# Spreading a row of token factors over the partitions: two small transfers through memory instead of a diagonal and matmuls with ones

## The chip, the cores and the metric

The kernel runs on one core of a Trainium2 chip. Its time is the device time of one launch in microseconds (us). The core has five engines with instruction streams of their own: TensorE (PE in the rows; PEld is its weight load), VectorE (DVE), ScalarE (ACT), GpSimd (POOL) and SyncE (SP), which here only issues transfers. They wait for one another by semaphores. Transfers between HBM and on-chip memory run on 16 DMA engines that all queues share; SP's transfers go out on one queue (q1) and those that GpSimd issues on another (q0).

## The reference, cut to what matters

Twelve sublayers follow one another on a stream `x` of 256 tokens by 1024 features, all in fp32. Each normalizes `x` by its root mean square, multiplies by matrices, normalizes the result and adds it to `x`:

```python
def rms_norm(x, g):
    y = x * rsqrt(mean(x * x, axis=-1, keepdims=True) + 1e-6)
    return y * g

# an FFN sublayer (8 of the 12); the others are one retention, one latent
# attention ("mla") and two mixers with stick-breaking attention ("stick")
h = rms_norm(x, g0)
f = (silu(h @ w_gate) * (h @ w_up)) @ w_down          # 1024 -> 2816 -> 1024
x = x + 0.5 * rms_norm(f, g1)
```

The factor `rsqrt(mean(x*x) + eps)` is one number for each token. It need not be applied to `h`: it may be applied after the first matrix product, since that product is linear in each token's row.

## The kernel before

**Layout.** The 256 tokens are two tiles (`T = 2`) of 128. Weights arrive in slots of 1 MB: `raw` holds three of them (`RING = 3`). For each slot ScalarE rounds it into `w_hi` (`high`, L929), VectorE takes the rest `raw - w_hi` into `w_lo` (`low`, L1317), and TensorE multiplies both parts, so that products of a two-part weight and a two-part activation (`h_hi`, `h_lo`) come near fp32. SP loads slot n + 3 once `low` of slot n is done. Every engine's stream is written out by hand in the order in which it runs; there is no planner.

**The token factor.** `h_hi` and `h_lo` hold `x` times the gain, without the token factor. ScalarE sums the squares of token tile t (`pre_sum`), GpSimd raises the mean to the power -0.5 (`pre_root`, L1825) into `stat[:, 4 + t]`, one number for each partition, tokens on partitions. Where a product has tokens on partitions, an engine applies the factor as a scalar of its instruction. Where a product has tokens along the row (`cols_of`, `gemm_pair`), the factor is needed as a row that is the same on all 128 partitions: `row_scale`, 128 x 256.

**How the row is made.** For the 11 sublayers that use it (all but the latent attention):
- VectorE, in `diag` (L1348): two 128 x 128 diagonals `row_diag` = identity times the factor, in the buffer `upd`. It is the last thing in `between`, the stretch between two sublayers; for sublayer 0 it stands before `low(6)`.
- TensorE, in `spread_scale` (L499): two fp32 matmuls of a matrix of ones with the diagonals, into `row_bank`, after the sublayer's first two slots (`first_slots`). They wait for `diag_ready`.
- ScalarE, in `row_copy` (L955): a copy of the bank to `row_scale`, after its `high(b + 3)` in an FFN sublayer, after the output of the second slot in the others.
- VectorE waits for `row_ready` before its first use: in an FFN sublayer the multiplication at L1502 in `gate(1)`, in the retention the scaling of the cosine table at L1631, in a stick sublayer the output of the third slot at L1731.

**An FFN sublayer on TensorE.** The first slots b and b + 1 (gate and up columns of chunk 0) come with tokens on partitions. Then `gemm_pair` on slot b + 2 (gate columns of chunk 1), four transposes at L680, `gemm_pair` on b + 3, `gemm_down` on b + 4, and a loop of chunks, each a gate pair, a down product and an up pair. The gate pair of chunk i + 1 waits for `gate_out` of chunk i, which VectorE gives at L1502.

**GpSimd's queue.** After the roots of sublayer 0 it computes the exponents of the retention's decay matrices, six times L1859, L1860 and L1861 on 128 x 512 elements, though they are not used before the retention. Then it loads gains. Between sublayers its order is: two roots of the update's norm (`post_root`), the load of the next `post_gain`, two roots of the next norm (`pre_root`), the load of `pre_gain` (L1832) for the sublayer after the next. In sublayer 0 VectorE computes the angles of the position tables (`angles`, L1446) between the first and the second chunk: 13 instructions, each waiting for the one before.

Of the kernel before, what the change touches and what calls it, by code (L numbers as in the profile page):

```python
# [17 lines left out]
P = 128  # L18
S = 256
T = S // P  # L20
# [77 lines left out]
def build(nc, ins, out):  # L98
# [3 lines left out]
    with ctx:  # L102
# [20 lines left out]
        row_scale = sb("row_scale", [P, S])  # L123
        row_diag = upd[:, 0:S].rearrange("p (a b) -> p a b", a=T)
        const = sb("const", [P, KEPT])
# [85 lines left out]
        up_parts = up_banks[:, :].rearrange("p (a b c) -> p a b c", a=2, b=2)  # L211
        row_bank, turn_bank = down[0][:, 0:S], down[1][:, 0:512]
        gemm_bank = [bank0, bank1]
# [16 lines left out]
        post_sq = sem("post_sq")  # L230
        diag_ready, row_mm, row_ready = sem("diag_ready"), sem("row_mm"), sem("row_ready")
        gate_side_out, gate_summed, up_side_out, up_out = (sem(n) for n in ("gate_side_out", "gate_summed", "up_side_out", "up_out"))
# [24 lines left out]
        pool_d, pool_mm, pool_hi, pool_lo = sem("pool_d"), sem("pool_mm"), sem("pool_hi"), sem("pool_lo")  # L257
        pool_w_zero = sem("pool_w_zero")

        block = ctx.enter_context(nc.Block())  # L260
# [143 lines left out]
        def _(pe):  # L404
# [93 lines left out]

            def spread_scale(u):  # L499

                pe.wait_ge(diag_ready, ROWS_BEFORE[u] + 1)
                for t in range(T):
                    last = mm(row_bank[:, t * P:(t + 1) * P], cst("ones"), row_diag[:, t, :], start=True, stop=True)
                last.then_inc(row_mm, 1)

            def down_of(n, k0, t, hi, lo, first, end, halves=range(2)):
# [152 lines left out]
            for u, kind in enumerate(SUBLAYERS):  # L659
                b = first_slot[u]  # L660
                if kind == "ffn":
                    e, g0, g1 = CHUNKS * ffns, (CHUNKS - 1) * ffns, (CHUNKS - 2) * ffns
                    first_slots(u + 1, [(b, bank0), (b + 1, bank1)], second=lambda: pe.wait_ge(evac, evacs[0]))
                    spread_scale(u)

# [31 lines left out]
                if kind == "ret":  # L697
                    mem = list(mem_heads(0, 0))
                    first_slots(u + 1, [(b + j, next_bank()) for j in range(2)])
                    spread_scale(u)  # L700
                    for j in range(2, N_RET):
# [86 lines left out]
                else:  # L788
# [35 lines left out]
                    first_slots(u + 1, [(b + j, next_bank()) for j in range(2)])  # L824
                    spread_scale(u)
                    for j in (2, 3):
# [80 lines left out]
        def _(sc):  # L907
# [43 lines left out]
            def scale_of(t):  # L951

                return stat[:, 4 + t:5 + t]

            def row_copy():  # L955

                rows[0] += 1
                sc.wait_ge(row_mm, rows[0])
                act_fn(row_scale[:, :], row_bank, ACT.Copy).then_inc(row_ready, 1)

            rows = [0]

# [123 lines left out]
            for u, kind in enumerate(SUBLAYERS):  # L1086
                b = first_slot[u]
                if kind == "ffn":
# [21 lines left out]
                    high(b + 3)  # L1110
                    row_copy()
                    high(b + 4)
# [30 lines left out]
                else:  # L1143
                    if kind == "ret":
# [19 lines left out]
                        for j in range(N_RET):  # L1164
                            steps((j, 0))
                            if 4 <= j < 10:

                                sc.wait_ge(slot_done, b + j + 1)
                                wait(sc, roped, j - 4)
                                bank = gemm_bank[evacs[0] % 2]  # L1170
                                act_fn(rope_sw[0:64, :], bank[64:P, :], ACT.Copy).then_inc(rope_swapped, 1)
                                act_fn(rope_sw[64:P, :], bank[0:64, :], ACT.Copy).then_inc(evac, 1)
                                evacs[0] += 1
                            elif j < 3:
                                rows_out(b + j, u, [(r_v[:, :, j * SC:(j + 1) * SC], 0, SC)])
                                if j == 1:
                                    row_copy()
# [68 lines left out]
                    else:  # L1246
                        c0 = 4 * sticks
                        for j in range(2):
                            rows_out(b + j, u, [(s_v[:, :, j * SC:(j + 1) * SC], 0, SC)])
                            if j == 1:  # L1250
                                row_copy()
                            high(b + j + 3)
# [60 lines left out]
        def _(ve):  # L1313
# [33 lines left out]

            def diag(u):  # L1348

                ve.wait_ge(pre_rs, 2 * (u + 1) + 2)  # L1350
                for t in range(T):
                    last = v.tensor_scalar(row_diag[:, t, :], ident, stat[:, 4 + t:5 + t], None, ALU.mult)
                last.then_inc(diag_ready, 1)

            def pre_low(p, t):
# [24 lines left out]
            def between(u):  # L1380
# [20 lines left out]
                low(b + 2)  # L1401
                if SUBLAYERS[u + 1] != "mla":
                    diag(u + 1)

# [78 lines left out]
            for t in range(T):  # L1483
                pre_low(1, t)
            diag(0)
            low(6)

            ffns, sticks = 0, 0
            for u, kind in enumerate(SUBLAYERS):
                b = first_slot[u]  # L1490
                if kind == "ffn":
                    e, g0, g1 = CHUNKS * ffns, (CHUNKS - 1) * ffns, (CHUNKS - 2) * ffns

                    def gate(i):
# [5 lines left out]
                        ve.wait_ge(gate_summed, g0 + i)  # L1500
                        ve.wait_ge(row_ready, ROWS_BEFORE[u] + 1)
                        v.tensor_tensor(sums, sums, row_scale[:, :].unsqueeze(1).broadcast_to([P, 2, S]), ALU.mult).then_inc(gate_out, 1)  # L1502
# [69 lines left out]
                else:  # L1572
                    if kind == "ret":
# [51 lines left out]
                        for j in range(N_RET):  # L1625
                            if j < 3:
                                low(b + j + 3)
                            if j == 1:
                                ve.wait_ge(table_ready, 1)
                                ve.wait_ge(row_ready, ROWS_BEFORE[u] + 1)  # L1630
                                v.tensor_tensor(trig[:, :, 0:S], trig[:, :, 0:S], row_scale[:, :].unsqueeze(1).broadcast_to([P, 2, S]),  # L1631
                                                ALU.mult).then_inc(trig_scaled, 1)
# [85 lines left out]
                    else:  # L1718
# [5 lines left out]
                        def slot_out(j):  # L1724
# [3 lines left out]
                            if j == 2:  # L1728
                                ve.wait_ge(row_ready, ROWS_BEFORE[u] + 1)
                            src = gemm_bank[(outs + j) % 2][:, :].rearrange("p (a b) -> p a b", a=2)  # L1730
# [87 lines left out]
        def _(gp):  # L1818
# [24 lines left out]
            def load_post_gain(u):  # L1843
                wait(gp, x_new, 4 * u)
                load_gain(post_gain, post_in, gain_row(u, 1))

            load_gain(post_gain, pre_in, ins["mem_norm"])
            gp.wait_ge(const_in, 16)
# [4 lines left out]
            for t in range(T):  # L1853
                pre_root(1, t)

            gp.wait_ge(small_in, SMALL_FIRST)
# [14 lines left out]
            for u, kind in enumerate(SUBLAYERS):  # L1871
# [65 lines left out]
```

## Time and profile before

| What | us |
|---|---|
| median of 3 runs (lowest and highest) | 1949.82 (1949.72 to 1950.51) |
| the profiled execution: its own time | 1949.68 |
| the profiled execution: span from first to last instruction | 1947.9 |
| TensorE busy (share of the span) | 1916.2 (98%) |
| VectorE busy | 1295.8 (67%) |
| ScalarE busy | 1032.6 (53%) |
| GpSimd busy | 158.4 (8%) |
| mean busy share of the DMA engines in the 40 slices of the span | 0.2 to 0.8, mostly 0.5 |

The granted clock of TensorE is at full speed in all 40 slices. Matmuls are pipelined and the profile models their ends, so the distance between starts tells more of their cost than the duration of one. "Idle" in the rows is time in which an engine stood still before an instruction, followed by what released it. In groups that name a line, a helper's line stands for all its callers.

### The profile page before, as it was taken

The numbers are of one execution on the slowest core, as the hardware profiler recorded it, in microseconds if no ns is written. First come the engines' busy times: TensorE is split into PE (matmuls) and PEld (weight loads), VectorE is DVE, ScalarE is ACT, GpSimd is POOL, SyncE is SP. The second block draws the span as 40 slices with busy tenths as digits, with TensorE's granted clock in tenths as the row PEclk, the third lists the DMA queues.
The fourth block names the chain that finished last, engine by engine and source line by source line (L and its number), as shares of the span: only waits on it lengthen the run. The fifth ranks groups of instructions, "written<-read, shape, count | busy, mean of one in ns | idle before, by whom it ended". The sixth has DMA issues, their size and how long they took to land.

```text
span 1947.9 us, 29001 instructions
## 1 busy us (share of the span) xinstructions
PE 1916.2 (98%) x11272; PEld 1685.9 (87%) x11272; DVE 1295.8 (67%) x1346; ACT 1032.6 (53%) x1190; POOL 158.4 (8%) x149
## 2 busy tenths in 40 slices
PE   6999999999999999999999999999999999999998
PEld 6888889888888887888888889888888888988887
DVE  4766756766676667666676666776667666667665
ACT  5544564544554457644464446654455445665443
POOL 2600113100000001100010001210001000300000
PEclk9999999999999999999999999999999999999999
DMA  8555553555555554455555556355555555535552
GB/s 303 195 194 194 179 164 134 195 194 193 175 201 186 190 167 139 145 203 194 188 180 196 190 187 205 112 192 197 191 194 195 173 193 196 195 130 182 184 187 104
DMA packets 262263, 356.25 MB, mean 183 GB/s; under 512 B 9008, under 2 KB 230576, under 8 KB 262192
## 3 DMA queue, kind: packets, MB, share of 16 engines
q1 hardware_dynamic: 258592, 342.15, 52.7%
q0 software_dynamic: 3600, 13.11, 1.8%
q8 instruction: 50, 0.82, 0.2%
q14 instruction: 21, 0.17, 0.0%
HBM read 354.19 MB, written 1.05 MB: 182 GB/s over the span
## 4 chain that ended last, share of the span: by engine, by line
PE 89%; DVE 4%; ACT 4%; issue 2%; DMA 1%; SPq 0%; POOL 0%; DVEq 0%; POOLq 0%; ACTq 0%
PE down L512 27%; PE gate_banks L435 15%; PE up_banks L435 14%; PE gate_banks L439 8%; PE up_banks L439 7%; PE up_banks L418 3%; PE up_banks L420 3%; PE up_banks L419 3%; PE up_banks L480 2%; ACT w_hi L940 1%; DVE w_lo L1327 1%; PE up_banks L471 1%; PE up_banks L472 1%; DVE xn L1345 1%; DMA raw<-in_ffn_w_gu 1%
## 5 line engine op out<-in xcount | busy, mean ns | idle before, releaser
L1321 DVE TENSOR_TENSOR w_lo<-raw,w_hi 128x2048 fp32r<-128x2048 f32 (+1 forms) x311 | 710.5, 2287 | 278.8 <-ACT w_hi L940 278.8
L940 ACT ACTIVATE w_hi<-raw 128x2048 fp32r<-128x2048 f32 x322 | 613.6, 1906 | 205.1 <-PE down L512 178.6
L435 PE MATMUL gate_banks<-h_both,w_hi 128*128 128x512 f32 x1280 | 321.0, 393 | 0.0
L435 PE MATMUL up_banks<-h_both,w_hi 128*128 128x512 f32 x1152 | 287.4, 391 | 0.0
L512 PE MATMUL down<-w_hi,m_hi 128*128 128x512 f32 x832 | 267.9, 394 | 0.0
L435 PEld LDWEIGHTS gate_banks<-h_both,w_hi 128*128 128x128 f32 x1280 | 230.6, 189 | 41.6
L512 PE MATMUL down<-w_lo,m_hi 128*128 128x512 f32 x832 | 264.8, 390 | 0.0
L512 PE MATMUL down<-w_hi,m_lo 128*128 128x512 f32 x832 | 264.4, 390 | 0.0
L435 PEld LDWEIGHTS up_banks<-h_both,w_hi 128*128 128x128 f32 x1152 | 211.1, 188 | 40.5
L439 PEld LDWEIGHTS gate_banks<-h_both,w_lo 128*128 128x128 f32 x1280 | 174.6, 190 | 12.5
L512 PEld LDWEIGHTS down<-w_hi,m_lo 128*128 128x128 f32 x832 | 156.2, 188 | 33.3
L512 PEld LDWEIGHTS down<-w_lo,m_hi 128*128 128x128 f32 x832 | 156.2, 188 | 33.1
L439 PE MATMUL gate_banks<-h_both,w_lo 128*128 128x256 f32 x1280 | 178.5, 282 | 0.0
L512 PEld LDWEIGHTS down<-w_hi,m_hi 128*128 128x128 f32 x832 | 150.8, 189 | 26.0 <-issue 0.3
L1093 ACT ACTIVATE big<-up_banks 128x512 f32<-128x512 f32 x72 | 43.3, 601 | 234.5 <-PE up_banks L439 234.5
L439 PEld LDWEIGHTS up_banks<-h_both,w_lo 128*128 128x128 f32 x1152 | 157.2, 190 | 11.2
L439 PE MATMUL up_banks<-h_both,w_lo 128*128 128x256 f32 x1152 | 160.6, 282 | 0.0
L418 PE MATMUL up_banks<-h_both,w_hi 128*128 128x256 f32 x512 | 147.2, 288 | 0.0
L419 PE MATMUL up_banks<-h_both,w_hi 128*128 128x256 f32 x512 | 144.8, 283 | 0.0
L420 PE MATMUL up_banks<-h_both,w_lo 128*128 128x256 f32 x512 | 144.8, 283 | 0.0
L1515 DVE TENSOR_TENSOR big<-up_banks,big 128x512 f32<-128x512 f32 x72 | 49.8, 691 | 123.0 <-ACT big L1093 123.0
L1829 POOL TENSOR_TENSOR stat<-stat,const 128x1 f32<-128x1 f32 x24 | 13.2, 552 | 1437.4 <-ACT stat L922 1437.4
(230 smaller groups left out, 2315.3 us busy)
## 6 DMA issues: line engine op xcount, KB each, us to landing
raw<-in_ffn_w_gu SPq DMA_DIRECT2D x88, 1024.0 KB, 5.0
raw<-in_ffn_w_down SPq DMA_DIRECT2D x88, 1024.0 KB, 4.9
raw<-in_ffn_w_gate SPq DMA_DIRECT2D x44, 1024.0 KB, 5.2
raw<-in_ffn_w_up SPq DMA_DIRECT2D x44, 1024.0 KB, 5.2
raw<-in_w_in SPq DMA_DIRECT2D x20, 1024.0 KB, 5.6
raw<-in_ret_w_in SPq DMA_DIRECT2D x13, 1024.0 KB, 5.2
raw<-in_w_o SPq DMA_DIRECT2D x8, 1024.0 KB, 4.9
raw<-in_w_out SPq DMA_DIRECT2D x8, 1024.0 KB, 4.7
```

The lines of the kernel that those rows point to most:

```text
L418: mm(o, w_hi[:, r, c:c + P], hi[:, k, :], start=(k == 0), stop=False)
L419: mm(o, w_hi[:, r, c:c + P], lo[:, k, :], start=False, stop=False)
L420: last = mm(o, w_lo[:, r, c:c + P], hi[:, k, :], start=False, stop=(k == KD - 1))
L435: mm(both, w_hi[:, r, c:c + P], h_both[:, k, :, :].rearrange("p a b -> p (a b)"), start=(k == 0), stop=(k == KD - 1), skip_group_check=True)
L439: last = mm(one, w_lo[:, r, c:c + P], h_hi[:, k, :], start=False, stop=(k == KD - 1), skip_group_check=True)
L471: mm(o, hi[:, k, ts], w_hi[:, n % RING, c:c + SC], start=(k == 0), stop=False)
L480: last = mm(o, hi[:, k, ts], w_lo[:, n % RING, c:c + SC], start=False, stop=(k == KD - 1))
L512: last = mm(down[t][:, c * 512:(c + 1) * 512], a[:, k0 + j, ts], w[:, r, j * D + c * 512:j * D + (c + 1) * 512], start=(first and j == 0 a ...
L940: act_fn(w_hi[:, r, 0:width], raw[:, r, 0:width], ACT.Copy).then_inc(hi_ready, 1)
L1093: act_fn(dst, parts[:, :, 1, :], ACT.Copy).then_inc(s, 1)
L1321: v.tensor_tensor(w_lo[:, r, 0:width], raw[:, r, 0:width], w_hi[:, r, 0:width].bitcast(f32), ALU.subtract).then_inc(lo_ready, 1)
L1515: v.tensor_tensor(sums, up_parts[:, :, 0, :], up_side, ALU.add).then_inc(up_out, 1)
```

## The change

The diagonals, the matmuls with ones and ScalarE's copy are gone, with their semaphores. In their place GpSimd issues two transfers, in `spread_rows`. The first writes the two columns of `stat`, 256 numbers on 128 partitions, to a row of 256 numbers in memory (HBM), 4 bytes at a time. GpSimd then waits for it to land (`row_put`) and issues the second, which reads that row of 1 KB onto each of the 128 partitions of `row_scale`. The consumers on VectorE stay where they were and wait for the second transfer.

```diff
-        row_diag = upd[:, 0:S].rearrange("p (a b) -> p a b", a=T)
...
+        row_store = nc.dram_tensor("row_store", (len(SUBLAYERS), S), f32, kind="Internal").ap()
...
-            def spread_scale(u):
-
-                pe.wait_ge(diag_ready, ROWS_BEFORE[u] + 1)
-                for t in range(T):
-                    last = mm(row_bank[:, t * P:(t + 1) * P], cst("ones"), row_diag[:, t, :], start=True, stop=True)
-                last.then_inc(row_mm, 1)
...
-            def row_copy():
-
-                rows[0] += 1
-                sc.wait_ge(row_mm, rows[0])
-                act_fn(row_scale[:, :], row_bank, ACT.Copy).then_inc(row_ready, 1)
...
-            def diag(u):
-
-                ve.wait_ge(pre_rs, 2 * (u + 1) + 2)
-                for t in range(T):
-                    last = v.tensor_scalar(row_diag[:, t, :], ident, stat[:, 4 + t:5 + t], None, ALU.mult)
-                last.then_inc(diag_ready, 1)
...
-                        ve.wait_ge(row_ready, ROWS_BEFORE[u] + 1)
+                        ve.wait_ge(row_ready, 16 * (ROWS_BEFORE[u] + 1))
...
+            def spread_rows(u):
+
+                gp.wait_ge(pre_rs, 2 * (u + 1) + 2)
+                gp.dma_start(row_store[u, :].rearrange("(t p) -> p t", p=P), stat[:, 4:4 + T], allow_slow_non_contiguous=True).then_inc(row_put, 16)
+                gp.wait_ge(row_put, 16 * (ROWS_BEFORE[u] + 1))
+                gp.dma_start(row_scale[:, :], row_store[u, :].partition_broadcast(P)).then_inc(row_ready, 16)
+
...
             for t in range(T):
                 pre_root(1, t)
+            spread_rows(0)
 
             gp.wait_ge(small_in, SMALL_FIRST)
             for h in range(HEADS_R):
...
                     pre_root(u + 2, 0)
                     pre_root(u + 2, 1)
+                if u + 1 < U and SUBLAYERS[u + 1] != "mla":
+                    spread_rows(u + 1)
                 if u + 2 < U:
                     load_pre_gain(u + 3)
```

The calls of `spread_scale`, `row_copy` and `diag` are removed at all their places. Two places in the instruction streams show what that does. On TensorE at the start of an FFN sublayer, before the change (L480 is the end of `first_slots`, L503 the matmuls with ones, L435 and L439 the first gate pair, L680 the transposes):

```order
L480 MATMUL up_banks<-w_lo,h_both 128x256 x8
L503 MATMUL down<-upd,const 128x128 x2
L435 MATMUL gate_banks<-h_both,w_hi 128x512 x8
L439 MATMUL gate_banks<-h_both,w_lo 128x256 x8
L435 MATMUL gate_banks<-h_both,w_hi 128x512 x8
L439 MATMUL gate_banks<-h_both,w_lo 128x256 x8
L680 MATMUL down<-const,big 128x128 x4
```

The same place after it:

```order
L481 MATMUL up_banks<-w_lo,h_both 128x256 x8
L436 MATMUL gate_banks<-h_both,w_hi 128x512 x8
L440 MATMUL gate_banks<-h_both,w_lo 128x256 x8
L436 MATMUL gate_banks<-h_both,w_hi 128x512 x8
L440 MATMUL gate_banks<-h_both,w_lo 128x256 x8
L673 MATMUL down<-const,big 128x128 x4
```

The two matmuls with ones are gone, and nothing else has moved. On GpSimd at the start of the program, between the roots of sublayer 0 and the decay exponents, before the change:

```order
L1832 DMA pre_gain<-in_norm_gains 128x1024 [waits pre_in]
L1825 TENSOR_TENSOR stat<-stat,const 128x1 [waits pre_ss] x2
L1859 TENSOR_SCALAR big<-big,lgd 128x512 [waits small_in]
L1860 TENSOR_SCALAR rope_t<-big,lgd 128x512
L1861 TENSOR_TENSOR big<-big,rope_t 128x512 [waits pool_link]
```

And after it:

```order
L1800 DMA pre_gain<-in_norm_gains 128x1024 [waits pre_in]
L1793 TENSOR_TENSOR stat<-stat,const 128x1 [waits pre_ss] x2
L1818 DMA row_store<-stat 128x2x1 [waits pre_rs]
L1820 DMA row_scale<-row_store 128x256 [waits row_put]
L1835 TENSOR_SCALAR big<-big,lgd 128x512 [waits small_in]
L1836 TENSOR_SCALAR rope_t<-big,lgd 128x512
L1837 TENSOR_TENSOR big<-big,rope_t 128x512 [waits pool_link]
```

The 18 instructions of the decay exponents now stand behind a wait for a transfer to land. At the other ten places the two transfers stand in the same way between the last root and the load of `pre_gain`.

## Rows read from the trace of the kernel before

**Rows 1.** Page, parts 1 and 4: busy time by engine; chain by engine.
```profile
PE 1916.2 (98%) x11272; PEld 1685.9 (87%) x11272; DVE 1295.8 (67%) x1346; ACT 1032.6 (53%) x1190; POOL 158.4 (8%) x149
...
PE 89%; DVE 4%; ACT 4%; issue 2%; DMA 1%; SPq 0%; POOL 0%; DVEq 0%; POOLq 0%; ACTq 0%
```
**Rows 2.** Waits of TensorE: line, releaser: us in total, times, longest.
```profile
PE up_banks L480 <- DVE w_lo L1327: 5.3, 11, 0.5
```
**Rows 3.** Chain that ended last, sublayer 3 (FFN): start us, us, what.
```profile
552.77 0.96 PE up_banks L480 x8
553.73 0.44 PE down L503 x4
554.18 1.85 PE gate_banks L435 x8
```
**Rows 4.** Timeline of GpSimd and VectorE, sublayer 3: start, us, engine, line, operation.
```profile
550.48 0.57 POOL L1832 DMA_DIRECT2D pre_gain<-in_norm_gains  x1
550.55 0.52 DVE L1352 TENSOR_SCALAR upd<-const,stat 128x128 f32<-128x128 f32 x2 [0.44 <-POOL stat L1825]
...
562.25 0.69 DVE L1502 TENSOR_TENSOR big<-big,row_scale 128x512 f32<-128x512 f32 x1
...
565.45 2.29 DVE L1321 TENSOR_TENSOR w_lo<-raw,w_hi 128x2048 fp32r<-128x2048 f32 x1 [2.50 <-ACT w_hi L940]
```
**Rows 5.** Timeline of TensorE, sublayer 3: start of the next chunk's gate pair.
```profile
571.11 1.98 PE L435 MATMUL gate_banks<-h_both,w_hi 128*128 128x512 f32 x8
```
**Rows 6.** Timeline, retention (first two) and first stick sublayer (last two).
```profile
240.06 0.57 POOL L1832 DMA_DIRECT2D pre_gain<-in_norm_gains  x1
...
250.97 0.68 DVE L1631 TENSOR_TENSOR trig<-trig,row_scale 128x512 f32<-128x512 f32 x1
...
1192.30 0.57 POOL L1832 DMA_DIRECT2D pre_gain<-in_norm_g  x1
...
1201.81 0.69 DVE L1731 SCALAR_TENSOR_TENSOR big<-up_banks,row_scale 128x512 f32<-128x512 f32 x1 [0.96 <-PE up_banks L420]
```
**Rows 7.** Page and DMA view, issues: count, KB each, median us to landing.
```profile
post_gain<-in_norm_gains POOLq DMA_DIRECT2D x6, 512.0 KB, 3.8
out<-x SPq DMA_DIRECT2D x4, 256.0 KB, 2.0
pos_row<-in_positions SPq DMA_DIRECT2D x1, 128.0 KB, 7.8
small<-in_conv_w SPq DMA_DIRECT2D x6, 1.0 KB, 4.5
pos_col<-in_positions SPq DMA_DIRECT2D x1, 1.0 KB, 7.6
```
**Rows 8.** Timeline of GpSimd and VectorE, sublayer 0: decay exponents and angles.
```profile
38.47 2.16 POOL L1859 TENSOR_SCALAR big<-big,lgd 128x512 f32<-128x512 f32 x1
...
64.41 1.57 POOL L1859 TENSOR_SCALAR big<-big,lgd 128x512 f32<-128x512 f32 x1
64.71 0.93 DVE L1502 TENSOR_TENSOR big<-big,row_scale 128x512 f32<-128x512 f32 x1
...
77.24 2.33 POOL L1861 TENSOR_TENSOR big<-big,rope_t 128x512 f32<-128x512 f32 x1
78.34 1.38 DVE L1450 CAST big<-pos_row 128x256 f32<-128x256 int32 x1
...
85.90 2.29 DVE L1321 TENSOR_TENSOR w_lo<-raw,w_hi 128x2048 fp32r<-128x2048 f32 x1
```
**Rows 9.** Timeline of TensorE, sublayer 0: the gate pair behind these angles.
```profile
90.15 2.00 PE L435 MATMUL gate_banks<-h_both,w_hi 128*128 128x512 f32 x8
```
**Rows 10.** Timeline, retention: GpSimd beside VectorE's tensor_scalar, and one alone.
```profile
265.03 1.31 POOL L1881 TENSOR_TENSOR big<-rope_t,rope_sw 128x512 f32<-128x512 f32 x1
265.43 1.33 DVE L1431 TENSOR_SCALAR big<-big,sm 128x256 f32<-128x256 f32 x2
...
268.68 0.62 DVE L1431 TENSOR_SCALAR big<-big,sm 128x256 f32<-128x256 f32 x2
```

More of the change, by code:

```diff
@@ L211, in build @@
         up_parts = up_banks[:, :].rearrange("p (a b c) -> p a b c", a=2, b=2)
-        row_bank, turn_bank = down[0][:, 0:S], down[1][:, 0:512]
+        turn_bank = down[1][:, 0:512]
         gemm_bank = [bank0, bank1]
@@ L230, in build @@
         post_sq = sem("post_sq")
-        diag_ready, row_mm, row_ready = sem("diag_ready"), sem("row_mm"), sem("row_ready")
+        row_put, row_ready = sem("row_put"), sem("row_ready")
         gate_side_out, gate_summed, up_side_out, up_out = (sem(n) for n in ("gate_side_out", "gate_summed", "up_side_out", "up_out"))
@@ L663, in _ @@
                     first_slots(u + 1, [(b, bank0), (b + 1, bank1)], second=lambda: pe.wait_ge(evac, evacs[0]))
-                    spread_scale(u)
                     def chunk(n, i, at=None):
@@ L699, in _ @@
                     first_slots(u + 1, [(b + j, next_bank()) for j in range(2)])
-                    spread_scale(u)
                     for j in range(2, N_RET):
@@ L824, in _ @@
                     first_slots(u + 1, [(b + j, next_bank()) for j in range(2)])
-                    spread_scale(u)
                     for j in (2, 3):
@@ L953, in scale_of @@
                 return stat[:, 4 + t:5 + t]
-            def row_copy():
-                rows[0] += 1
-                sc.wait_ge(row_mm, rows[0])
-                act_fn(row_scale[:, :], row_bank, ACT.Copy).then_inc(row_ready, 1)
-            rows = [0]
             def pre_high(p, t):
@@ L1110, in _ @@
                     high(b + 3)
-                    row_copy()
                     high(b + 4)
@@ L1175, in _ @@
                                 rows_out(b + j, u, [(r_v[:, :, j * SC:(j + 1) * SC], 0, SC)])
-                                if j == 1:
-                                    row_copy()
                             elif j == 3:
@@ L1249, in _ @@
                             rows_out(b + j, u, [(s_v[:, :, j * SC:(j + 1) * SC], 0, SC)])
-                            if j == 1:
-                                row_copy()
                             high(b + j + 3)
@@ L1401, in between @@
                 low(b + 2)
-                if SUBLAYERS[u + 1] != "mla":
-                    diag(u + 1)
             def head_low(head, banks=early):
@@ L1484, in _ @@
                 pre_low(1, t)
-            diag(0)
             low(6)
@@ L1629, in _ @@
                                 ve.wait_ge(table_ready, 1)
-                                ve.wait_ge(row_ready, ROWS_BEFORE[u] + 1)
+                                ve.wait_ge(row_ready, 16 * (ROWS_BEFORE[u] + 1))
                                 v.tensor_tensor(trig[:, :, 0:S], trig[:, :, 0:S], row_scale[:, :].unsqueeze(1).broadcast_to([P, 2, S]),
@@ L1728, in slot_out @@
                             if j == 2:
-                                ve.wait_ge(row_ready, ROWS_BEFORE[u] + 1)
+                                ve.wait_ge(row_ready, 16 * (ROWS_BEFORE[u] + 1))
                             src = gemm_bank[(outs + j) % 2][:, :].rearrange("p (a b) -> p a b", a=2)
```

## The prediction

> **What bounds the kernel now.** I read the page first, for who is busy. TensorE is busy for 1916.2 of 1947.9 us, and the chain of work that ended last runs on it for 89% [rows 1]: a microsecond taken from TensorE's stream is a microsecond of the kernel, unless something else then arrives late. Then TensorE's waits, for how close the others are. At the eleven boundaries between sublayers it waits 5.3 us in all for VectorE's half slots, at most 0.5 us at one place [rows 2]. Inside the sublayers its starts follow one another without gaps. Then the chain at the place of the change: the matmuls with ones stand in it directly between the last product of `first_slots` and the first gate product [rows 3]. The timelines of VectorE and GpSimd give the time from the last root to the first reader of `row_scale` [rows 4, 6]. Sublayer 0 I read apart, since only there GpSimd has other work behind the inserted transfers [rows 8].
>
> **What TensorE gains.** The chain gives the pair of fp32 matmuls (four records) 0.44 us [rows 3]. Nothing takes their place: the gate pair behind them needs slot b + 2, whose low part VectorE had finished before it turned to the diagonals at 550.55, 3 us before TensorE comes to them [rows 3, 4]. There are 8 FFN, 1 retention and 2 stick sublayers, so 11 x 0.44 = 4.8 us. The first gate product after the switch back from fp32 also starts a hundredth slower (1.85 us there); I take 4.9 us. The bounds are 0, if each pair's time were lost again at the next boundary, and 6.6 us, if each were worth its whole modelled duration of some 0.6 us. The chain is a row at this very place, so I stay by it. The removed diagonals (0.52 us on VectorE) and the copy on ScalarE were beside TensorE's work, and VectorE stands still behind them until TensorE ends a slot: 0, in either direction.
>
> **What the two transfers need, and what they have.** No row shows a store of 4-byte pieces or a read behind it. Nearest for the first is the load of 1 KB in 4-byte pieces, 4.5 us; its bounds are the large store of `out`, 2.0, and the 4-byte load in the flood of the start, 7.6. For the second, GpSimd's broadcast of 512 KB takes 3.8, and `pos_row`, the same shape as here but in that flood, 7.8 [rows 7]. Between ends so far apart I take 4.5 + 3.8 = 8.3 us, because the flood is over by then; both ends, 2.0 + 3.8 = 5.8 and 7.6 + 7.8 = 15.4, are kept.
>
> They start where `pre_gain` is loaded now. In an FFN sublayer that is 550.48, and VectorE reads the row at 562.25: 11.8 us [rows 4]. If it comes later, L1502, the rounding of the next slot and VectorE's low part, which ends at 565.45 + 2.29 = 567.74, move with it. TensorE wants them at 571.11 [rows 4, 5], so 3.4 us more are to be had, 15.1 in all. In the retention the reader comes 10.9 us after the start, in the stick sublayer 9.5 us [rows 6]. Behind that stick reader TensorE has another slot to multiply into the other bank, 48 products of 0.12 us (8 in 0.96, rows 3), 5.8 us more. So 8.3 us are hidden at all eleven places, 15.4 us would cost some tenths at each, about 3 us in all. I take 0.
>
> What queues behind GpSimd's wait: between sublayers only the load of `pre_gain`, which is issued some 5 us later and is first read a whole sublayer later. It will then share the DMA engines with another weight slot than now. The slots have one sublayer's pace of slack and the load takes 3.8 us alone [rows 7], so nothing.
>
> **Sublayer 0.** Here the 18 instructions of the decay exponents wait for the first transfer. They began at 38.47 [rows 8]; now they begin some 4.5 us later (2.0 to 7.6). One group of three takes 1.57 for each of the two `tensor_scalar` [rows 8] and 1.31 for a `tensor_tensor` of this size [rows 10], 4.4 us. So GpSimd runs one group late, and its last group, which ended at 77.24 + 2.33 = 79.57, falls under `angles`, VectorE's 13 dependent instructions that begin at 78.34 and keep the next gate waiting. The rows show what that costs. The `CAST` at 78.34 took 1.38 us and ended just after GpSimd's instruction [rows 8]; two `tensor_scalar` beside a GpSimd instruction took 1.33 instead of 0.62, and again ended as it did [rows 10]. Only L1502 beside a GpSimd `tensor_scalar` got off with 0.93 instead of 0.69 [rows 8 and 4]. So VectorE loses between 0.2 us and the whole of each GpSimd instruction that gets in. All three: 4.4 us, less the 1.2 us that the `CAST` pays already, 3.2 us. The low part of the slot behind the angles ends at 85.90 + 2.29 = 88.19; TensorE wants it at 90.15 [rows 8, 9], 0.45 us earlier now. The margin is 1.5 us. TensorE stalls 3.2 - 1.5 = 1.7 us, once, and does not get it back, since it bounds all that follows. The bounds: 0 when only tenths are lost, and 4.4 + 3.1 - 1.2 - 1.5 = 4.8 us when the first transfer takes 7.6 and the whole delay of GpSimd falls on VectorE.
>
> The Trainium skill, SBUF — State Buffer, section Who interferes with whom, says that a VectorE instruction in a two-port mode and a GpSimd instruction exclude each other for the whole instruction, and that a VectorE instruction with two SBUF inputs is held by a GpSimd instruction that reads SBUF. By that rule all three instructions count in full, and the stall is 1.7 us or more. The `CAST` and the paired `tensor_scalar` agree with it, L1502 beside the `tensor_scalar`, held for 0.24 us only, does not.
>
> **The sum.** 1949.68 (the profiled execution, 1.8 above its span and 0.14 below the median of the runs) - 4.9 + 0 + 1.7 = 1946.5 us. Its own range, with the stall from 0.5 to 3.2, is 1945.2 to 1948.0.
>
> **The rivals.**
> - Clean saving. GpSimd's delay is absorbed before the angles, or its instructions get in between VectorE's without holding them beyond the margin of 1.5 us: 1949.7 - 4.9 = 1944.8. For it speaks L1502's small loss, and that GpSimd's instructions also stretch wherever VectorE keeps it out. Against it, that the last group ended only at 79.57 with no delay at all.
> - The saving does not arrive. TensorE comes 0.44 us earlier to each boundary and waits there for VectorE's half slot that much longer [rows 2]; with the stall of sublayer 0 the time is 1949.7 to 1951.4. Against it: those half slots follow from TensorE's own last products, so they move with it.
> - Slower, by one mechanism: the pair of transfers outlasts the slack and VectorE's wait at L1502 holds up the gate pair of the second chunk in each FFN sublayer. It decides from 15.1 us for the pair on; each microsecond above costs 11, since the other three places have about as much, and 15.6 us take back the whole gain. At 20 us, if each transfer waited out a weight slot in flight, the time is 1949.7 - 4.9 + 11 x 4.9 = 1999. For it speaks that both 1 KB loads of the start took 7.6 and 7.8 [rows 7]; against it, that in the flood they had several megabytes in front of them.
>
> **How the numbers follow.** My forecast has 0.57, the clean saving 0.27, the lost saving 0.08, the outlasted slack 0.08. A change under 0.2%, 3.9 us, can't be told from none here: the border is 1945.9. The forecast's range reaches across it, with about 0.13 of its chance; with the clean saving that makes faster 0.40. Within 0.2% are the rest of the forecast, 0.44, and 0.07 of the lost saving and 0.01 of a barely outlasted slack: 0.52. Slower has 0.08. The range: 1944.5 takes in the clean saving, and 1948.6 the forecast with the stall at 3.7 and a little over; above it stay the lost saving and the slower case with part of the bound of 4.8.
>
> **What would show it.** Right: four records fewer between `first_slots` and the gate pair at each of the eleven places, and the next product 0.44 us sooner; no idle time of VectorE before L1502's successor put down to a transfer; both transfers landed within 8 us or so; in sublayer 0 decay exponents that still run at 80 us, a span of the angles longer than now, and TensorE idle for 1 to 3 us before the gate pair near 90 us. Wrong: idle time before the first reader of `row_scale` released by a transfer, or a sublayer 0 that is shorter by 0.44 us like the others; then the stall was priced too high. If the boundaries grow, the saving was no saving.

## The result

| Kernel | us, median (lowest to highest) | span of the profiled execution | mean granted clock in it |
|---|---|---|---|
| before | 1949.94 (1949.61 to 1950.51, 6 runs) | 1947.9 | 1.000 |
| after | 2002.92 (1998.35 to 2004.02, 6 runs) | 2000.4 | 0.988 |

The change made the kernel slower: the ratio is 1.0269, 95% interval 1.0259 to 1.0279. The prediction of 1946.5 us was wrong, in sign and far outside its range. What happened is its last rival, to which it gave 0.08.

### The profile page after: what moved, and what is told of

It is laid out like the page before. It is cut to its first block, busy times and chain, and to the rows that moved or that the text cites. A ratio compares the mean times of both kernels' runs of the same rounds, so it can differ in the third digit from the quotient of the medians.

```text
span 2000.4 us, 28902 instructions
## 1 busy us (share of the span) xinstructions
PE 1932.7 (97%) x11228; PEld 1696.4 (85%) x11228; DVE 1292.6 (65%) x1324; ACT 1027.6 (51%) x1179; POOL 172.4 (9%) x171
## 4 chain that ended last, share of the span: by engine, by line
PE 80%; DMA 9%; DVE 4%; ACT 4%; issue 2%; POOL 1%; DVEq 0%; SPq 0%; POOLq 0%; ACTq 0%
PE down L506 25%; PE gate_banks L436 14%; PE up_banks L436 12%; PE gate_banks L440 7%; PE up_banks L440 6%; DMA row_store<-stat 5%; DMA row_scale<-row_store 3%; PE up_banks L419 3%; PE up_banks L420 2%; PE up_banks L421 2%; DVE w_lo L1299 1%; PE up_banks L472 1%; PE up_banks L473 1%; POOL stat L1793 1%; ACT w_hi L931 1%
## 5 line engine op out<-in xcount | busy, mean ns | idle before, releaser
L436 PE MATMUL gate_banks<-h_both,w_hi 128*128 128x512 f32 x1280 | 332.4, 403 | 25.5 <-DVE w_lo L1299 25.5
L436 PEld LDWEIGHTS gate_banks<-h_both,w_hi 128*128 128x128 f32 x1280 | 237.9, 195 | 72.3 <-DVE w_lo L1299 28.7
L419 PE MATMUL up_banks<-h_both,w_hi 128*128 128x256 f32 x512 | 149.8, 292 | 9.6 <-DVE big L1699 9.6
L420 PE MATMUL up_banks<-h_both,w_hi 128*128 128x256 f32 x512 | 147.1, 287 | 0.0
```

What stands on the lines that cost most here:

```text
L419: mm(o, w_hi[:, r, c:c + P], hi[:, k, :], start=(k == 0), stop=False)
L420: mm(o, w_hi[:, r, c:c + P], lo[:, k, :], start=False, stop=False)
L436: mm(both, w_hi[:, r, c:c + P], h_both[:, k, :, :].rearrange("p a b -> p (a b)"), start=(k == 0), stop=(k == KD - 1), skip_group_check=True)
```

## The profile after

The page, parts 1 and 4, against [rows 1]:

```profile
PE 1932.7 (97%) x11228; PEld 1696.4 (85%) x11228; DVE 1292.6 (65%) x1324; ACT 1027.6 (51%) x1179; POOL 172.4 (9%) x171
...
PE 80%; DMA 9%; DVE 4%; ACT 4%; issue 2%; POOL 1%; DVEq 0%; SPq 0%; POOLq 0%; ACTq 0%
```

TensorE has 44 records fewer and yet 16.5 us more of busy time, so some of its work ran slower. The chain has a new member, DMA with 9%, taken from PE. The DMA issues of the two transfers (count, KB each, median us to landing) stand against [rows 7]:

```profile
row_scale<-row_store POOLq DMA_DIRECT2D x11, 128.0 KB, 6.6
row_store<-stat POOLq DMA_DIRECT2D x11, 1.0 KB, 10.8
```

The store alone takes longer than the prediction gave the pair. From the issue of the store to the landing of the read it is 17.0 to 18.5 us at the eleven places. The waits (who for whom: us in total, times, longest) show where that ends, beside [rows 2]:

```profile
POOL row_scale L1820 <- DMA row_store<-stat: 114.7, 11, 11.2
DVE big L1470 <- DMA row_scale<-row_store: 48.4, 7, 7.4
PE gate_banks L436 <- DVE w_lo L1299: 25.5, 8, 3.9
DVE big L1699 <- DMA row_scale<-row_store: 21.1, 2, 10.7
...
PE up_banks L419 <- DVE big L1699: 9.6, 2, 4.9
...
PE up_banks L481 <- DVE w_lo L1305: 5.3, 11, 0.5
```

The last row is [rows 2] unchanged: the boundaries are what they were. The third one is new, and so is the one of L419, the same wait in the two stick sublayers. In the retention TensorE stands still for 1.30 us at a place where it did not before (L566). Sublayer 3 as a timeline, against [rows 4, 5]:

```profile
560.61 0.75 POOL L1818 DMA_DIRECT2D row_store<-stat  x1 [0.29 <-POOL stat L1793]
571.48 0.57 POOL L1820 DMA_DIRECT2D row_scale<-row_store  x1 [10.12 <-DMA row_store<-stat]
578.96 0.69 DVE L1470 TENSOR_TENSOR big<-big,row_scale 128x512 f32<-128x512 f32 x1 [7.39 <-DMA row_scale<-row_store]
582.15 2.29 DVE L1299 TENSOR_TENSOR w_lo<-raw,w_hi 128x2048 fp32r<-128x2048 f32 x1 [2.50 <-ACT w_hi L931]
584.50 3.65 PE L436 MATMUL gate_banks<-h_both,w_hi 128*128 128x512 f32 x8 [3.87 <-DVE w_lo L1299]
588.96 2.00 PE L436 MATMUL gate_banks<-h_both,w_hi 128*128 128x512 f32 x8
```

The chain is the one that the prediction drew: store, read, L1470 (L1502 before), the rounding, the low part, the gate pair. The row arrives 18.3 us after the store's issue, 3.2 more than the slack of 15.1. TensorE idles 3.87 us, and then its first eight products take 3.65 us instead of 2.00. The windows of the same place (PE, PEld, DVE, ACT, POOL busy; then granted clock, DMA share, GB/s) say why:

```profile
565.00:570.00 5.00, 5.00 (x33) 4.54 (x32) 3.93 (x2) 1.39 (x3) 0.00 (x0) 1.00 0.53 26
...
580.00:585.00 5.00, 1.13 (x5) 0.59 (x4) 2.85 (x3) 4.40 (x4) 0.00 (x0) 0.97 0.15 53
585.00:590.00 5.00, 5.00 (x21) 4.14 (x20) 4.96 (x6) 2.44 (x2) 0.00 (x0) 0.69 0.67 216
590.00:595.00 5.00, 5.00 (x28) 4.27 (x27) 3.37 (x4) 2.92 (x3) 0.00 (x0) 1.00 0.97 341
```
```profile
586.00:588.00 2.00, 2.00 (x7) 1.51 (x6) 2.00 (x2) 1.59 (x2) 0.00 (x0) 0.50 0.96 326
```

After the idle time the granted clock is at 0.50 (1.2 GHz), and then at full speed again. The first row holds the other surprise. While the store is under way, the DMA engines are busy for 0.53 of the time and move 26 GB/s. The weight slot issued in that time, and the one behind it, landed after 9.4 and 12.8 us instead of some 5.

The lengths of the sublayers (from one first `post_root` to the next, minus those of before, in us) show how even the loss is. I use them for the experiments too:

```
sublayer      0     1     2     3     4     5     6     7     8     9    10    11
kind        ffn   ret   ffn   ffn   mla   ffn   ffn stick   ffn   ffn stick   ffn
after      1.72  2.42  5.65  5.30  0.02  5.60  6.17  6.56  4.96  3.97  6.06  3.85
```

They sum to 52.3; the spans differ by 52.5. The latent attention, which uses no row, has not changed.

## The experiments

Runs of before beside the timed ones had medians of 1949.95 to 1950.10 us. "Theory A" is that the store is slow by itself, wherever it is issued, and that the wait for the row is the loss.

**The store from ScalarE's queue.** In `spread_rows` the store goes; ScalarE issues it at the end of `between`:

```diff
-                gp.dma_start(row_store[u, :].rearrange("(t p) -> p t", p=P), stat[:, 4:4 + T], ...).then_inc(row_put, 16)
+                sc.dma_start(row_store[u, :].rearrange("(t p) -> p t", p=P), stat[:, 4:4 + T], ...).then_inc(row_put, 16)
```

> The kernel after, but ScalarE's queue issues the store of 256 four-byte pieces, at the same point of time; the read stays with GpSimd. Theory A (the store itself is slow to land, whoever issues it): the store still lands 10 to 11 us after its issue, GpSimd waits about as long, time 1995 to 2005. Rival B (GpSimd's queue makes it slow): it lands in 4 to 5 us as the 4-byte loads of before did, the pair needs 11 to 12 us, less than the slack of 15.1, and the time is 1945 to 1950.

Measured: 1993.12 us, ratio 1.0223 (1.0206 to 1.0240). Its DMA issues:

```profile
row_scale<-row_store POOLq DMA_DIRECT2D x11, 128.0 KB, 6.8
row_store<-stat ACTq DMA_DIRECT2D x11, 1.0 KB, 10.4
```

The store lands as late, so the queue is not the cause. The 10 us gained are more than theory A allowed. The pairs take 17.5 us on average instead of 17.9, and ScalarE issues the store some 0.3 us earlier against TensorE's stream. In the seven FFN sublayers 2 to 11 the second gate pairs come 19.6 us later in sum where they came 25.0 us later in the kernel after, and the slow clock behind them costs 10.3 us instead of 13.5. That is 8.5 of the 10.8 us between the two spans.

**The store alone, and the pair, beside the old way.** The kernel before keeps its diagonals and matmuls; GpSimd issues the store as well, in the second kernel both transfers into a spare buffer:

```diff
+                gp.dma_start(row_store[u, :].rearrange("(t p) -> p t", p=P), stat[:, 4:4 + T], ...).then_inc(row_put, 16)
+                gp.wait_ge(row_put, 16 * (ROWS_BEFORE[u] + 1))                            # the second kernel only
+                gp.dma_start(spare, row_store[u, :].partition_broadcast(P)).then_inc(...)  # the second kernel only
```

> The kernel before, its diagonals, matmuls with ones and copy kept, and GpSimd issues the store as well, which nobody reads (it waits for it before the next post_root only). If the store holds up the weight transfers enough to matter by itself (theory A2), slots issued beside it land in 9 to 13 us, ScalarE waits for them, and the time is 1955 to 1975. If all the harm comes by the wait for the row (theory A1): 1949 to 1952, with late slots that nobody misses.

> The kernel before, its own way to the row kept, and both transfers issued by GpSimd as in the kernel after, with its wait between them; they fill a spare buffer that nobody reads. A1 (the wait for the row is all): 1950 to 1953, of which about 2 are sublayer 0, where GpSimd's decay exponents start 11 us later and meet the angles. A2 (interference with the weights, or the later load of pre_gain): 1960 or more.

Measured: 1950.88 us (ratio 1.0004, 0.9995 to 1.0014) and 1951.78 us (1.0009, 0.9999 to 1.0018). The store still lands after 10.9 and 10.6 us, and the DMA issue rows of the first kernel at sublayer 3 show weights and gain late beside it:

```profile
raw<-in_ffn_w_gu SPq DMA_DIRECT2D x2, 1024.0 KB, 9.1
raw<-in_ffn_w_down SPq DMA_DIRECT2D x1, 1024.0 KB, 9.4
pre_gain<-in_norm_gains POOLq DMA_DIRECT2D x1, 512.0 KB, 11.6
row_store<-stat POOLq DMA_DIRECT2D x1, 1.0 KB, 11.6
```

No sublayer grows by more than 0.13 us with the store and, beyond sublayer 0 (0.54), by 0.10 with the pair. So late weights by themselves cost next to nothing here: the loss is the wait for the row, with what follows from it.

**Pieces of 8 bytes.** The row is stored token-major, 128 pieces of 8 bytes; VectorE reads it with a stride, in two instructions for each one of the kernel after:

```diff
-                gp.dma_start(row_store[u, :].rearrange("(t p) -> p t", p=P), stat[:, 4:4 + T], ...)
+                gp.dma_start(row_store[u, :].rearrange("(p t) -> p t", t=T), stat[:, 4:4 + T])
```

> The kernel after, with the row stored token-major, as 128 pieces of 8 bytes in place of 256 of 4; VectorE reads row_scale with a stride of 8 bytes, in two instructions for each one of after. If the store's landing time goes by the piece (the pieces landing one after another, some 21 ns each), it falls from 10.8 to about 8 us, the pair to 15.5, at the slack of 15.1, and the time is 1946 to 1965. If it is a fixed time, 10.8 stays and the time is 1998 to 2008.

Measured: 1948.93 us, ratio 0.9993 (0.9983 to 1.0003), 54 us less than after. The store takes 6.0 to 7.1 us until the read is issued, the pair 11.3 to 14.5. The longest pair, at sublayer 3, tests the slack of 15.1 and outlasts it: VectorE waits 3.62 us, TensorE stands still for 0.18 before the gate pair, which starts 0.34 us later for it and takes 2.12 instead of 1.98. This sublayer is 0.04 us longer than before where most are 0.45 shorter.

```profile
558.30 0.54 POOL L1831 DMA_DIRECT2D row_scale<-row_store  x1 [6.55 <-DMA row_store<-stat]
565.74 0.76 DVE L1299 TENSOR_TENSOR big<-big,row_scale 128x256 f32<-128x256 f32 x2 [3.62 <-DMA row_scale<-row_store]
571.36 2.12 PE L436 MATMUL gate_banks<-h_both,w_hi 128*128 128x512 f32 x8 [0.18 <-DVE w_lo L1306]
```

**Forms of the store, and of the read.** Two kernels with the old way to the row and, at each boundary, one transfer that nobody needs. The edit is that of the first; the second reads the 256 positions, a row of 1 KB, onto 128 partitions, in turn from GpSimd's and ScalarE's queue:

```diff
-                gp.dma_start(row_store[u, :].rearrange("(t p) -> p t", p=P), stat[:, 4:4 + T], ...)
+                dst, src = stores[PLAN[u]]              # another form at each boundary
+                gp.dma_start(dst, src, ...)
```

> The kernel before, and at each of the twelve boundaries one unneeded store from GpSimd's queue at the place of after's, of another form: 256, 512 and 128 pieces of 4 bytes, 128 pieces of 8 bytes, 256 pieces of 4 bytes set 64 or 512 bytes apart, 128 pieces of 64 bytes, one piece of 1 KB, and 128 pieces of 8 bytes into on-chip memory. By the piece: 512 pieces land after 15 to 17 us, 256 after 10.8 however far apart, 128 after about 8, one piece after about 5. By the line of memory that neighbouring pieces share: those 512 bytes apart land as fast as one piece. Fixed: all land near 10.8. The time stays within 1949.5 to 1953.

> The kernel before, and at each boundary one unneeded read of a row of 1 KB onto 128 partitions, without a store ahead of it: in turn from GpSimd's queue and from ScalarE's. If the store makes the read behind it slow, GpSimd's read lands in 3.8 to 4.5 us here and not in 6.6. If the read is as slow by itself, beside a weight slot, 6 to 7 us. ScalarE's queue: 3 to 5 us if GpSimd's queue is what delays the first packet, as long as GpSimd's if it is the slot in flight. The time stays within 1949.5 to 1953.

Issues of the store kernel. The trace leaves digits out of names: `p256x`, `p512x` and `p128x` of 0.5 KB are pieces of 4 bytes, `p128x` of 1 KB pieces of 8 bytes, of 8 KB pieces of 64 bytes, `apart` pieces of 4 bytes 64 and 512 bytes apart, `pos_row` the on-chip target.

```profile
p256x<-const POOLq DMA_DIRECT2D x2, 1.0 KB, 9.8
p128x<-const POOLq DMA_DIRECT2D x2, 1.0 KB, 7.3
p512x<-const POOLq DMA_DIRECT2D x2, 2.0 KB, 11.1
apart<-const POOLq DMA_DIRECT2D x2, 1.0 KB, 5.2
p128x<-const POOLq DMA_DIRECT2D x1, 0.5 KB, 9.8
one1k<-const POOLq DMA_DIRECT2D x1, 1.0 KB, 6.0
p128x<-const POOLq DMA_DIRECT2D x1, 8.0 KB, 5.4
pos_row<-const POOLq DMA_DIRECT2D x1, 1.0 KB, 5.3
```

"By the piece" falls: 128 pieces of 4 bytes take as long as 256, and the same 256 pieces take half as long when they lie 64 bytes apart or more. "Fixed" falls too. What makes the store slow is that its 4-byte pieces lie close together in HBM. The trace's DMA packets narrow down where the time goes. In the kernel after, the 16 packets on record for a store take at most 0.03 us each and the last one begins 3.3 to 6.7 us after the issue; then 3.7 to 7.4 us pass until the landing is told. In the kernel of store forms it is 4.2 to 6.6 us for the touching 4-byte pieces, 0.7 and 3.0 for the pieces of 8 bytes and 0.4 to 0.8 for all other forms. So the extra time lies behind the last packet.

The read of 1 KB onto 128 partitions took a median of 5.8 us from GpSimd's queue and 5.5 from ScalarE's, without a store ahead of it; in the kernel after it took 6.6. So the read is slow by itself, mostly, and the queue hardly matters. Times: 1950.87 and 1951.03 us, one run each.

**How close is close.** The same kernel, with other gaps and widths, and a second time with repeats of the forms in between:

```diff
-        PLAN = [the forms above]
+        PLAN = ["touching", "gap_eight", "gap_sixteen", "gap_thirtytwo", "piece_sixteen", "gap_sixtyfour", ...]
```

> The kernel before with one unneeded store at each of the twelve boundaries, as in the earlier kernel of store forms: 256 pieces of 4 bytes that touch, or begin 8, 16, 32 or 64 bytes apart, and 128 pieces of 16 or 32 bytes that touch. Theory L (pieces that fall into the same 64 bytes of memory wait for one another, about 0.29 us each, while different 64 bytes go side by side): over the 5.2 us of pieces 64 bytes apart, 16 pieces in 64 bytes add 4.6 us (landing 9.8), 8 (gap of 8) 2.3 (7.5), 4 (gap of 16, pieces of 16) 1.2 (6.4), 2 (gap of 32, pieces of 32) 0.6 (5.8). Rival (any piece under 64 bytes is slow where it touches its neighbour, gaps of any width are free): touching 4-byte pieces 9.8, all gaps 5.2, pieces of 16 and 32 bytes 6 to 8.

> The kernel before with one unneeded store at each boundary, again, for repeats of the forms in between: 256 pieces of 4 bytes that touch (two places), 128 pieces of 8 bytes that touch (four), 256 pieces of 4 bytes that begin 8 bytes apart (three) and 16 bytes apart (three). If only the number of pieces in the same 64 bytes counts (16, 8, 8 and 4), pieces of 8 bytes and gaps of 8 land alike, about 6.8 us, and gaps of 16 in 5.5 to 6. If it counts that pieces touch, pieces of 8 bytes land in 6.7 to 8 and both gaps in 5 to 6.4. Touching 4-byte pieces: 9.3 to 10.3 in both.

Each landing of the three kernels, in us, by how many pieces fall into the same 64 bytes of HBM:

```
pieces in 64 bytes   form                              landings
16                   4 bytes, touching (128 to 256)    9.3 9.3 9.4 9.7 9.8 10.3 10.7
 8                   8 bytes, touching                 5.8 6.0 6.2 6.6 6.7 7.9
 8                   4 bytes, every 8                  5.8 5.8 6.3 6.4 7.1
 4                   4 bytes every 16; 16 bytes        4.9 5.2 5.3 5.8 6.9; 4.5 5.3
 1 or 2              4 bytes every 32, 64, 512;        4.9 5.5 4.6 4.8 5.9;
                     32 or 64 bytes                    6.0; 5.4
```

Pieces of 8 bytes and gaps of 8 are alike (medians 6.4 and 6.3), so it is not that pieces touch: the number that share a neighbourhood counts. Theory L as I had put it, 0.29 us for each piece, does not hold: over the median of 5.3 us of the last two groups, 16 pieces add 4.4, 8 add 1.0, and 4 nothing that stands out of the spread of 2.4 us. What is awaited behind the last packet these traces don't show, nor whether 64 bytes is the unit. Times: 1951.70 and 1950.68 us, one run each.

**Filling the idle time.** The kernel after, with products that nobody reads in the place of the idle time:

```diff
+                    if u:
+                        pe.wait_ge(gate_summed, g0 + 1)
+                        for k in range(16):
+                            mm(bank6, h_both[:, k % 8, 0, 0:P], h_both[:, k % 8, :, :]..., start=True, stop=True, ...)
+                    chunk(b + 2, 1, at=b + 5)
```

> The kernel after, with 16 products of 512 columns that nobody reads put on TensorE ahead of the second gate pair of the seven later FFN sublayers, where it stands idle for the row; the second chunk is taken out of the loop on TensorE for that. The wait stays as long, it is only filled. Theory D (each idle time of about 4 us is followed by a stretch at 1.2 GHz that costs 1.7 to 3.4 us more): the half-clock stretches of these sublayers go, and the time falls by 13 to 20 us, to 1983 to 1990. If the clock costs nothing beside the wait: 2000 to 2006.

Measured: 1986.39 us, ratio to before 1.0189 (1.0171 to 1.0208), 16.5 us less than after. Timeline of TensorE, sublayer 3, to be held against 3.87 and 3.65 above:

```profile
574.53 3.79 PE L681 MATMUL gate_banks<-h_both 128*128 128x512 f32 x16
578.16 2.04 PE L436 MATMUL gate_banks<-h_both,w_hi 128*128 128x512 f32 x8
```

The FFN sublayers 2 to 11 are 3.17 to 3.46 us longer than before, which is the filler less the 0.44 saved. The gate pair follows it at full clock. In the kernel after the same sublayers are 3.85 to 6.17 longer. The difference, 12.9 us over the seven, is about what the slow clock takes beside the wait, since the filler delays each gate pair by 3.6 us, as the wait did on average. The starts of the kernel after agree: its seven gate pairs come 25.0 us later in sum, and 13.5 us more are lost behind them. The mean granted clock rises from 0.988 to 0.997. The rest of the 16.5 us lies in sublayers that the filler doesn't touch (0, 1, 7 and 10), where the pairs happened to be shorter by 0.4 to 1.7 us.

**The row in on-chip memory, and sublayer 0.** The kernel after with the row in one partition of on-chip memory, as two stores of 128 pieces of 4 bytes; in the second kernel GpSimd does its wait and the read of sublayer 0 after the first of six groups of decay exponents:

```diff
-                gp.dma_start(row_store[u, :].rearrange("(t p) -> p t", p=P), stat[:, 4:4 + T], ...).then_inc(row_put, 16)
+                for t in range(T):
+                    gp.dma_start(row_line(u)[:, t * P:(t + 1) * P].rearrange("o (p c) -> o p c", c=1), stat[:, 4 + t:5 + t]).then_inc(row_put, 16)
...
-                gp.dma_start(row_scale[:, :], row_store[u, :].partition_broadcast(P)).then_inc(row_ready, 16)
+                gp.dma_start(row_scale[:, :], row_line(u).unsqueeze(1).broadcast_to([1, P, S])).then_inc(row_ready, 16)
```

> The kernel after, but the row goes to one partition of on-chip memory instead of HBM, in two stores of 128 pieces of 4 bytes, and the second transfer reads it from there onto 128 partitions. Theory L: with no piece waiting at a line of HBM the stores land in 5.3 to 6 us, the read in 5 to 6.5, the pair in 11 to 12.5, under the slack of 15.1; the time is 1945.5 to 1948, what is left over the clean saving of 1945 being sublayer 0's stall. If small pieces are slow wherever they go, the pair stays above 15.1 and the time is over 1955.

> As the kernel with the row in on-chip memory, and in sublayer 0 GpSimd does its wait and the read only after the first of the six groups of decay exponents, so that they start with the issue of the stores and not after their landing. If the delay of these exponents is what costs sublayer 0 its 2 us, the time is 1 to 2.2 us less than that kernel's, 1944.5 to 1946, and TensorE does not stand idle before the gate pair near 90 us. If sublayer 0's loss has another cause: no difference.

Measured: 1947.14 us, ratio 0.9987 (0.9978 to 0.9996), and 1947.71 us, 0.9988 (0.9979 to 0.9997). The first is the best version here, 0.13% faster than before. Its DMA issues, its waits, and its chain by engine:

```profile
row_scale<-pos_row POOLq DMA_DIRECT2D x10, 128.0 KB, 6.6
pos_row<-stat POOLq DMA_DIRECT2D x20, 0.5 KB, 5.0
```
```profile
DVE big L1468 <- DMA row_scale<-pos_row: 12.8, 7, 2.4
...
PE up_banks L479 <- DVE w_lo L1303: 5.3, 11, 0.5
```
```profile
PE 90%; ACT 3%; DVE 3%; issue 2%; DMA 0%; POOL 0%; SPq 0%; DVEq 0%; POOLq 0%; ACTq 0%
```

With pairs of 10.9 to 13.3 us VectorE waits a little, TensorE not at all, and nine of the eleven sublayers with a row are 0.43 to 0.46 us shorter than before, sublayer 0 is 0.52 and sublayer 5 is 0.17: the saving is there, 4.7 us in sum.

The span is only 3.6 us shorter, for 1.1 us is lost behind TensorE's last product. GpSimd's stream ends with a `DRAIN`, and in this kernel the program ends with it. It takes 2.72 us in the kernel before, where GpSimd issues 25 transfers, 3.62 with 36 (the kernel with the unneeded store), 4.52 with 47 (the kernel after) and 5.41 with 58 here, 0.08 us more for each transfer. In the kernel before, it is over 1.8 us before the program ends and costs nothing.

The later read in sublayer 0 gained nothing, and there was nothing left to gain, as sublayer 0 had lost nothing in the first kernel. The exponents started at 40.05 instead of 44.11 and their last instruction began at 81.22 instead of 81.11, since VectorE's instructions stretched GpSimd's (two took 5.60 and 3.48 us that take 1.57 alone) and 0.9 us went to the wait for the stores and the issue of the read.

## Why the prediction was wrong

**The bound that failed.** The step is "Between ends so far apart I take 4.5 + 3.8 = 8.3 us, because the flood is over by then; both ends [...] 7.6 + 7.8 = 15.4, are kept." Measured: 10.8 + 6.6 and the issue between them, 17.0 to 18.5 us, above even the upper end. The sentence behind it, "So 8.3 us are hidden at all eleven places", fell with it. The rows I priced the store by were loads of 4-byte pieces into on-chip memory [rows 7]. It is a store of 4-byte pieces into HBM, and where the pieces go is what matters: 4.6 to 5.9 us at 64 bytes or more apart, 5.0 on chip, 9.3 to 10.7 touching in HBM. The only row of a store to HBM had large pieces. The read was also under-priced, 6.6 instead of 3.8, and its like without a store took 5.8, "the flood" or not.

The Trainium skill, DMA: Bandwidth & Descriptors, section Specifications, says that transfers under 512 bytes make the DMA engine read, modify and write. By that rule alone the touching pieces and those 512 bytes apart would cost alike; here they take 9.8 and 5.9 us. Its section Anatomy of one DMA puts most of a fixed cost of about 2 us on the wait for the target memory's receipt. The place agrees: 3.7 to 7.4 us of this store lie behind its last packet. The figure does not, since the store took 10.8 us, five times as long.

**What the prediction had right.**
- TensorE's gain: 0.44 us at each place. The best version shows 0.43 to 0.46 at nine of eleven and 4.7 in all sublayers, with 4.8 forecast for the eleven. Its span is 3.6 below that of before, for the reason given there.
- The chain from L1502 to the second gate pair, and nearly the slack of 15.1 us. TensorE's idle times there, with the pair's length in the same sublayer, are 3.08 (17.5), 3.87 (18.3), 3.91 (18.3), 3.70 (18.1), 3.81 (18.2), 2.77 (17.2) and 2.65 (17.0): 14.4 us less in each. An idle time counts from an end that the profile models. By the starts, which came 3.24, 4.04, 4.08, 3.87, 3.97, 2.93 and 2.82 us later, the slack was 14.2 us in each. The pair of 14.5 in the kernel with 8-byte pieces fits it: 0.34 later, 0.07 of that through VectorE's longer multiplication. Of the missing 0.9, 0.44 is the time by which TensorE now comes earlier, which I had counted as gain and not taken from the slack.
- That queued loads behind GpSimd's wait cost nothing: `pre_gain` came 11 us later and nobody waited; the pair beside the old way cost no sublayer but the first over 0.10.

**The term that was missing.** The rival priced the outlasted slack at 11 us for each microsecond above 15.1. With an average pair of 17.9 it gives 1949.7 - 4.9 + 11 x 2.8 = 1976 (with the true slack of 14.2, 1985), and 2003 was measured. Its price counts the wait alone. Each idle time, 2.65 to 3.91 us in the FFN sublayers, was followed by a stretch at 1.2 GHz, and filling seven of them took 12.9 us off those sublayers. TensorE had no idle time of this size before, so no row priced it ("without gaps" was too smooth, though: the latent attention had idle times of up to 1.28 us and the stick sublayers of 0.91, all at full clock); but a rival in which TensorE stands still needs such a term, left open if no row has it.

**Sublayer 0** lost as I had forecast in kind, and the size was partly luck. I had 1.7 us for a delay of GpSimd of 4.5. In the kernel after the delay was 12.1, and TensorE stood still before that gate pair, as the timeline shows:

```profile
89.39 2.28 DVE L1299 TENSOR_TENSOR w_lo<-raw,w_hi 128x2048 fp32r<-128x2048 f32 x1
91.73 2.11 PE L436 MATMUL gate_banks<-h_both,w_hi 128*128 128x512 f32 x8 [1.74 <-DVE w_lo L1299]
```

With pieces of 8 bytes (delay 7.9) it was 1.45, in the kernel with the unneeded pair 0.29, and with the row on chip (delay 5.6) nothing. The exponents ended at 88.9, 86.5, 87.7 and 82.4 us in these four, so neither the delay nor the end alone sets the price. What the price does follow is the length of the angles, 9.4, 9.0, 8.4 and 7.6 us in the four against 6.3 before. Which instructions meet decides that, and the rule of it stays open. My sum let the angles grow by the whole of a group, 3.2 us, at a delay of 4.5; at 5.6 they grew by 1.3. Ahead of the angles GpSimd gave way (5.20 us for an instruction of 1.57 in the kernel after). Under them VectorE did: GpSimd's last six took 1.30 to 1.72 us, hardly more than alone.

**The chances.** The rival that came true had 0.08 because "in the flood they had several megabytes in front of them". That explained away the two largest rows I had, 7.6 and 7.8 us. A cost for which no row exists, bounded by rows of another direction, deserved more weight on the far side, and its upper end of 15.4 already lay above the 15.1 from which it decides.

## What to carry to other kernels

- A store is priced by a store to the same memory with pieces of the same size, never by a load. Neighbouring 4-byte pieces to HBM took 9.3 to 10.7 us and held other transfers up; the same bytes as 8-byte pieces, spaced, or on chip took 4.3 to 7.9.
- A slack read from a timeline held to 0.9 us. What was wrong was the thing put into it. When a price has no row of its own, compare the slack with twice the upper bound before calling it hidden.
- Where TensorE stands still for some 4 us, add the slow clock behind it: here some 1.8 us beside 3.4 of idle time, for each.
- Count the transfers that GpSimd issues. Each made the end of its stream 0.08 us longer, which cost 1.1 us with 58 of them.

## What the runs showed of the hardware

- Touching 4-byte pieces stored to HBM held up other traffic: a window of 5 us with the DMA engines 0.53 busy at 26 GB/s, the two weight slots issued there landed after 9.4 and 12.8 us instead of some 5. Stores of the same pieces set 64 or 512 bytes apart did not: single 4 KB packets of the slots beside them took at most 1.5 us, beside the touching ones up to 4.5 to 6.2.
- The number of pieces hardly counts: 128, 256 and 512 touching pieces landed after 9.8, 9.3 to 10.7, and 11.0 to 11.3 us. From ScalarE's queue 256 took 10.4. In the kernel after, 3.7 to 7.4 us of it passed behind the last packet.
- Other tiny stores beside weight slots mostly took 4.5 to 6 us: one piece of 1 KB to HBM 6.0, and 128 pieces of 8 bytes to on-chip memory 5.3.
- After idle times of TensorE of 2.65 to 4.94 us the granted clock stood at 0.50 for 3.4 or 6.8 us, nine times in the kernel after, and once after 1.30 us, in the retention. The length alone does not decide: with the store from ScalarE's queue an idle time of 2.69 us and one of 1.51 us were not followed by it, and one of 2.10 us was. With products in the idle time it did not fall.
- The `DRAIN` at the end of GpSimd's stream took 2.72, 3.62, 4.52 and 5.41 us with 25, 36, 47 and 58 transfers issued by GpSimd.
